# Gate and up projections of a decoder layer: a fourth pair of k-tiles by seven block products in every other chunk

## The chip, the cores and the metric

The kernel runs on one core of a Trainium2 chip. The metric is the device time of one execution in microseconds (us). Engines are called PE (TensorE matmul), PEld (its weight load), DVE (VectorE), ACT (ScalarE), POOL (GpSimd) and SP (SyncE, which here issues the weight DMAs).

## What is computed

One layer of a hybrid decoder on 256 tokens and 2048 channels, in float32: a half-step SwiGLU feed-forward (FFN), a token mixer (state-space branch and windowed attention, merged and projected), and a second SwiGLU FFN, each followed by a LayerNorm. The change touches the first half of both FFNs:

```python
def swiglu(x, w_gate, w_up, w_down):
    return (jax.nn.silu(x @ w_gate) * (x @ w_up)) @ w_down
# D_MODEL = 2048, FFN_HIDDEN = 5632, SEQ = 256, all float32
h = layer_norm(ALPHA * h + 0.5 * swiglu(h, ffn1_w_gate[l], ffn1_w_up[l], ffn1_w_down[l]), ...)
mix = hybrid_mixer(h, ...)
h = layer_norm(ALPHA * h + mix, ...)
h = layer_norm(ALPHA * h + 0.5 * swiglu(h, ffn2_w_gate[l], ffn2_w_up[l], ffn2_w_down[l]), ...)
```

## The kernel before

**Three products for one.** A float32 product is made of three products of rounded parts. For rows `a` and weights `w` the kernel keeps `a_hi`, `a_lo`, `w_hi`, `w_lo` (the rounded value and the rest) and adds `hi*hi + hi*lo + lo*hi` into one PSUM bank. The helper `three` issues these three matmuls, each 128 rows of one token tile by 512 columns.

**Slabs.** Weights stream as slabs of 128 x 2 x 512 (512 KB). SP loads slab n into one of four landing slots (`load`, the DMA is at L540) once the split of slab n-4 is done. ACT rounds it into one of four `w_hi` slots (L1395) when PE has used slab n-4, DVE subtracts to get `w_lo` (L1853) and increments `rest`, on which PE waits. All engines walk through the slabs in the same written-out order.

**Chunks.** The hidden width of 5632 is cut in 11 chunks of 512 columns. A chunk takes 16 slabs: eight pairs of k-tiles, b = 0 to 7, each once for gate and once for up. Chunk 0 (`up_first`) is done with all slabs plain, 12 matmuls each, while the input rows are still being transposed and split on the way in. Chunks 1 to 10 (`up_seven`) do the pairs b in `SEVEN = (2, 4, 6)` by seven block products, the others plainly (24 matmuls a pair).

**Seven products.** Two k-tiles, two token tiles, and gate and up form a 2x2 by 2x2 block product. `seven_products` makes it of 7 products of three matmuls, 21 matmuls instead of 24: two on slab l, two on slab l+1, and three on block sums of the weights. Four bank pairs serve: `own` is the chunk's own PSUM tensor, `aux` the other one (`acc` and `spare` in turn). It needs

- on the rows' side four sums and differences of the row blocks (`s_hi`, `s_lo`), made once per FFN in `up_first`: `mixed_rows`, which is `mixed_of` (L2037 to L2043, on DVE), then `mixed_high` (L1498, ACT), then `mixed_low` (L2071, DVE). They go one set at a time through the scratch rows `sz`, at l = 10, 12 and 14;
- on the weights' side three sums per block: `block_sums` (L2080, L2083, L2085, on DVE) before the two splits, then their rounded part `t_hi` (L1519, ACT, waits until PE has used the previous block's, `t_used`) and the rest `t_lo` (L2090, DVE, increments `t_rest`). There is one `t_hi`/`t_lo`.

**Chunk ends.** At the start of the next chunk ACT copies one shared bank (L1524), `collect` (L2096 to L2098, DVE) takes the shared `aux` banks apart, `sum_chunk` (L2013, L2015) and `product_summed` (L2020) finish the hidden values, PE transposes them (L925), and ACT and DVE split them into `g_hi` (L1477) and `g_lo` (L2028). PE starts a chunk only when `collect` of the previous chunk has freed the banks (`banks_drained`).

**Loops.** Chunks 1 and 2 stand in the open (`ALONE = 2`), chunks 3 to 10 in a loop of four turns with two chunks each; SP has one loop over chunks 1 to 10. In FFN 1, DVE's part of chunk 0 also holds `columns` at l = 7 (small copies of parameters) and `angles` at l = 9 (17 small operations for the rotary positions).

Of the kernel before, what the change touches and what calls it, by code (L numbers as in the profile page):

```python
# [22 lines left out]
ALU = mybir.AluOpType  # L23
# [60 lines left out]

SEVEN = (2, 4, 6)
NC_S = 10
# [9 lines left out]
              for j in range(2)]  # L96
UP_BLOCKS = NC_S * len(SEVEN)
ALL_BLOCKS = UP_BLOCKS + sum(DOWN_BLOCKS)
# [12 lines left out]
MIXED = FFN_MIXED + len(WSO_SEVEN[0])  # L111
ALONE = 2 - NC_S % 2
HIDDEN_AT = 6
# [110 lines left out]

def seven_block(f, i, b):
    return i * len(SEVEN) + ((f - 1) * ALL_BLOCKS - len(SEVEN)) + SEVEN.index(b)

# [75 lines left out]
def build_decoder_layer(nc, x, positions, ffn1_w_gate, ffn1_w_up, ffn1_w_down, ln1_g, ln1_b, w_in, conv_w, conv_b,  # L303
# [20 lines left out]
    with ctx:  # L324
# [201 lines left out]
        def _(sp):  # L526
# [249 lines left out]
        def _(pe):  # L776
# [156 lines left out]

            def seven_products(n, slab_at, l, rows_of, mixed, own, aux, first, last, turned=None):
# [23 lines left out]
            def up_seven_block(f, i, b, own, aux):  # L958
# [103 lines left out]

            def up_seven(f, i, odd):

                own, aux = chunk_banks(odd), chunk_banks(1 - odd)
                banks_drained(f, i)
                for b in range(8):
                    if b == SEVEN[0] and isinstance(i, int) and i == 1:
                        pe.wait_ge(mix_out, (f - 1) * MIXED + len(SEVEN))
                    if b in SEVEN:  # L1070
                        up_seven_block(f, i, b, own, aux)
# [314 lines left out]
        def _(act):  # L1386
# [134 lines left out]
            def copy_one(f, i, odd):  # L1521

                act.wait_ge(t_used, seven_block(f, i, SEVEN[-1]) + 1)
                act.activation(q_one, chunk_banks(1 - odd)[:, 0, :], ACT.Copy).then_inc(q_copied, 1)  # L1524

            def up_seven(f, i, odd):

                for l in range(16):
                    if l == 4 and not (isinstance(i, int) and i == 1):
                        silu_summed(f, i - 1)  # L1530
                    if l == 1 and not (isinstance(i, int) and i == 1):
                        copy_one(f, i - 1, 1 - odd)
                    if l == HIDDEN_AT:
                        hidden_high(f, i - 1, 1 - odd)
                    n = seven_block(f, i, l // 2) if l // 2 in SEVEN else None
                    if n is not None and l % 2 == 0:
                        act.wait_ge(sums, n * 3 + 1)
                    split(f"up{f}", i, l)
                    if n is not None and l % 2 == 1:
                        t_high_part(n)  # L1540

            def ffn(f, ln, cols):
                up_first(f, ln, cols)
                for i in range(1, ALONE + 1):
                    up_seven(f, i, i % 2)
                with act.Fori(1, 1 + (NC_S - ALONE) // 2) as m:
                    for k in range(2):
                        up_seven(f, m * 2 + (ALONE - 1 + k), (ALONE + 1 + k) % 2)
                down(f)
# [8 lines left out]
            def down(f):  # L1558
                for j in range(2):
                    for l, (p, c) in enumerate(DOWN_SLABS[j]):  # L1560
                        s = DOWN_ORDER[j][p]
                        if j == 0 and l == 1:
                            copy_one(f, NC_S, NC_S % 2)
                        if j == 0 and l == 4:
# [282 lines left out]
        def _(dve):  # L1847
# [238 lines left out]

            def t_low_part(n):

                dve.wait_ge(t_high, n + 1)
                dve.tensor_tensor(t_lo[:, :, :], t_sums, t_hi[:, :, :].bitcast(F32), ALU.subtract).then_inc(t_rest, 1)  # L2090

# [25 lines left out]

            def up_seven(f, i, odd):
                for l in range(16):
# [604 lines left out]
```

## Time and profile before

| | us |
|---|---|
| median of 3 runs | 2651.9 (2651.47 to 2652.64) |
| the profiled execution, its own time | 2653.86 |
| span of the profiled execution | 2652.3 |
| PE busy | 2625.4 (99%), 12519 matmuls |
| PEld busy | 2178.3 (82%) |
| DVE busy | 2081.2 (78%) |
| ACT busy | 1378.4 (52%) |
| POOL busy | 128.6 (5%) |
| granted PE clock, mean | 0.998 |

The profile is of one execution. Start times count from the start of its span. In the timeline a row is start, duration, engine, line, operation, what is written from what, how often in a row, and, where the engine was idle before it, how long and who released it. A busy share is an average over the whole span; where an engine is late is seen only in the timeline of one chunk. A matmul's duration is its latency and not what it costs in a row of matmuls: its start to the next one's start is.

### The profile page before, as it was taken

To read this page: it belongs to the slowest core of one execution; us is meant where nothing else is said; L and a number is where in the kernel's file an instruction comes from. 1 tells how busy PE (TensorE), PEld (TensorE's weight loads), DVE (VectorE), ACT (ScalarE), POOL (GpSimd) and SP (SyncE) were. 2 spreads that over 40 slices of the span, in tenths; PEclk is the share of its full clock that TensorE was granted. 3 is DMA by queue.
4 is the path that set the end of the run, shared out by engine and by line. 5 is a ranking of instruction groups with operands and counts; after the bars stand their busy time and mean duration, and the time that the engine had idled before them with its cause. 6 is when DMAs were issued, how large, how long until landed. Compare 5 with 4: busy or idle time off the path is not lost.

```text
span 2652.3 us, 35957 instructions
## 1 busy us (share of the span) xinstructions
PE 2625.4 (99%) x12519; PEld 2178.3 (82%) x12519; DVE 2081.2 (78%) x2372; ACT 1378.4 (52%) x1663; POOL 128.6 (5%) x170
## 2 busy tenths in 40 slices
PE   9999999999999999999999999999999999999997
PEld 7888888888887788888888888788888888888886
DVE  6989989798666665677777765887788989897986
ACT  4555555454444454555665554454465555554553
POOL 1000000000000000211111100000000000000000
PEclk9999999999999999999999999999999999999999
DMA  7666666766655545665655565656666666667564
GB/s 222 196 198 205 192 203 197 229 200 199 200 174 146 158 148 194 206 182 177 185 178 175 177 179 177 210 199 210 212 209 201 190 207 193 202 197 256 190 211 170
DMA packets 286471, 514.03 MB, mean 194 GB/s; under 512 B 19664, under 2 KB 53120, under 8 KB 284320
## 3 DMA queue, kind: packets, MB, share of 16 engines
q1 hardware_dynamic: 279824, 485.03, 58.7%
q0 software_dynamic: 4880, 25.36, 2.6%
q10 hardware_dynamic: 1664, 2.26, 0.2%
q8 instruction: 65, 1.06, 0.2%
q14 instruction: 38, 0.31, 0.0%
HBM read 506.23 MB, written 6.36 MB: 193 GB/s over the span
## 4 chain that ended last, share of the span: by engine, by line
PE 92%; DVE 5%; ACT 1%; DMA 1%; issue 1%; ACTq 0%; POOLq 0%; POOL 0%; SPq 0%; DVEq 0%
PE acc L826 11%; PE acc L828 11%; PE acc L827 11%; PE acc L930 5%; PE acc L932 5%; PE acc L931 5%; PE spare L930 5%; PE spare L931 5%; PE spare L932 5%; PE acc L912 4%; PE acc L913 4%; PE acc L914 4%; PE spare L914 3%; PE spare L912 3%; PE spare L913 3%; PE spare L795 2%
## 5 line engine op out<-in xcount | busy, mean ns | idle before, releaser
L1853 DVE TENSOR_TENSOR w_lo<-land,w_hi 128x1024 fp32r<-128x1024 f32 (+1 forms) x956 | 1150.6, 1222 | 408.2 <-ACT w_hi L1395 399.9
L1395 ACT ACTIVATE w_hi<-land 128x1024 fp32r<-128x1024 f32 (+1 forms) x956 | 965.7, 1026 | 892.9 <-DVE land L2080 293.8
L826 PE MATMUL acc<-w_hi,a_hi 128*128 128x512 f32 (+1 forms) x1168 | 444.1, 380 | 1.8 <-DVE w_lo L1853 1.7
L828 PE MATMUL acc<-w_hi,a_lo 128*128 128x512 f32 (+1 forms) x1168 | 428.8, 367 | 0.0
L827 PE MATMUL acc<-w_lo,a_hi 128*128 128x512 f32 (+1 forms) x1168 | 427.5, 366 | 0.0
L826 PEld LDWEIGHTS acc<-w_hi,a_hi 128*128 128x128 f32 x1168 | 220.4, 189 | 46.2 <-issue 11.0
L828 PEld LDWEIGHTS acc<-w_hi,a_lo 128*128 128x128 f32 x1168 | 220.2, 189 | 37.4
L827 PEld LDWEIGHTS acc<-w_lo,a_hi 128*128 128x128 f32 x1168 | 220.6, 189 | 36.8 <-issue 3.8
L912 PE MATMUL acc<-w_hi,a_hi 128*128 128x512 f32 x512 | 201.6, 394 | 0.7 <-DVE w_lo L1853 0.7
L914 PE MATMUL acc<-w_hi,a_lo 128*128 128x512 f32 x512 | 199.5, 390 | 0.0
L913 PE MATMUL acc<-w_lo,a_hi 128*128 128x512 f32 x512 | 199.5, 390 | 0.0
L2090 DVE TENSOR_TENSOR t_lo<-land,t_hi 128x1536 fp32r<-128x1536 f32 x91 | 159.3, 1751 | 0.3 <-ACT t_hi L1519 0.2
L912 PE MATMUL spare<-w_hi,a_hi 128*128 128x512 f32 x400 | 156.5, 391 | 0.0
L914 PE MATMUL spare<-w_hi,a_lo 128*128 128x512 f32 x400 | 155.8, 389 | 0.0
L913 PE MATMUL spare<-w_lo,a_hi 128*128 128x512 f32 x400 | 155.6, 389 | 0.0
L1519 ACT ACTIVATE t_hi<-land 128x1536 fp32r<-128x1536 f32 x91 | 134.0, 1473 | 0.0
L2080 DVE TENSOR_TENSOR land<-land 128x1024 f32<-128x1024 f32 x91 | 111.0, 1220 | 19.8 <-DMA land<-ffn_w_down 9.8
L930 PE MATMUL spare<-w_hi,g_hi 128*128 128x512 f32 x292 | 114.1, 391 | 0.8 <-DVE w_lo L1853 0.8
L912 PEld LDWEIGHTS acc<-w_hi,a_hi 128*128 128x128 f32 x512 | 96.3, 188 | 21.3 <-DVE w_lo L1853 1.1
L930 PE MATMUL acc<-w_hi,g_hi 128*128 128x512 f32 x292 | 113.7, 389 | 0.0
L932 PE MATMUL spare<-w_hi,g_lo 128*128 128x512 f32 x292 | 113.7, 389 | 0.0
L932 PE MATMUL acc<-w_hi,g_lo 128*128 128x512 f32 x292 | 113.6, 389 | 0.0
(448 smaller groups left out, 4360.9 us busy)
## 6 DMA issues: line engine op xcount, KB each, us to landing
land<-w_in SPq DMA_DIRECT2D x232, 512.0 KB, 3.7
land<-ffn_w_gate SPq DMA_DIRECT2D x176, 512.0 KB, 3.8
land<-ffn_w_up SPq DMA_DIRECT2D x176, 512.0 KB, 4.0
land<-ffn_w_down SPq DMA_DIRECT2D x176, 512.0 KB, 4.6
land<-w_ssd_o SPq DMA_DIRECT2D x64, 512.0 KB, 4.4
land<-w_in SPq DMA_DIRECT2D x132, 128.0 KB, 2.3
land<-w_attn_o SPq DMA_DIRECT2D x32, 512.0 KB, 3.8
land<-w_out SPq DMA_DIRECT2D x32, 512.0 KB, 4.7
```

What stands on the lines that cost most here:

```text
L826: pe.matmul(to, rows_hi, hi, start=first, stop=False)
L827: pe.matmul(to, rows_hi, lo, start=False, stop=False)
L828: mm = pe.matmul(to, rows_lo, hi, start=False, stop=last)
L912: pe.matmul(to, rows_hi, hi, start=first and k == 0, stop=False)
L913: pe.matmul(to, rows_hi, lo, start=False, stop=False)
L914: mm = pe.matmul(to, rows_lo, hi, start=False, stop=last and k == 1)
L930: pe.matmul(to, rows[0], block[0], start=first, stop=False)
L931: pe.matmul(to, rows[0], block[1], start=False, stop=False)
L932: return pe.matmul(to, rows[1], block[0], start=False, stop=last)
L1395: act.activation(w_hi[:, l % SPLIT, 0:deep, 0:width], land[:, l % LAND, 0:deep, 0:width], ACT.Copy).then_inc(high, 1)
L1853: dve.tensor_tensor(w_lo[:, l % SPLIT, 0:deep, 0:width], land[:, l % LAND, 0:deep, 0:width], w_hi[:, l % SPLIT, 0:deep, 0:width].bitcast(F ...
L2090: dve.tensor_tensor(t_lo[:, :, :], t_sums, t_hi[:, :, :].bitcast(F32), ALU.subtract).then_inc(t_rest, 1)
```

## The change

In chunks 1 to 8 the odd ones ("four") take pairs 2, 4, 5, 6 by seven block products, the even ones ("three") 2, 4, 6 as before; chunks 9 and 10 ("last") are as before. There is a second `t_hi`/`t_lo`, and the blocks of chunks 1 to 8 alternate between the two. A fourth set of mixed rows is made in `up_first`, so that `mixed_rows` now stands at l = 8, 10, 12 and 14, ahead of the split of its slab, `mixed_high` at l = 9, 11, 13 and 15 and `mixed_low` two slabs behind its `mixed_rows`. The loop has three turns (chunks 3 to 8), and chunks 9 and 10 stand in the open behind it, on SP also. Waits are the same, with new counts; `t_hi` waits for the block before the previous one where the set allows it. The core of the diff:

```diff
-SEVEN = (2, 4, 6)
+SEVEN = (2, 4, 5, 6)
+UP_SEVEN = {"four": (2, 4, 5, 6), "three": (2, 4, 6), "last": (2, 4, 6)}
+UP_T_SET = {"four": (0, 1, 0, 1), "three": (0, 1, 0), "last": (0, 0, 0)}
+UP_T_FREE = {"four": (0, 1, 1, 1), "three": (1, 1, 1), "last": (0, 0, 0)}
+LOOPED = 8
...
-        s_hi = [placed(f"s_hi{k}", [P, 4, P], F32R, at * K) for k, at in enumerate((88, 90, 92))]
-        s_lo = [placed(f"s_lo{k}", [P, 4, P], F32R, at * K) for k, at in enumerate((94, 86, 42))]
+        s_hi = [placed(f"s_hi{k}", [P, 4, P], F32R, at * K) for k, at in enumerate((88, 90, 92, 40))]
+        s_lo = [placed(f"s_lo{k}", [P, 4, P], F32R, at * K) for k, at in enumerate((94, 86, 42, 84))]
+        t_sets = [(t_hi, t_lo), (placed("t_hi_two", [P, 3, W], F32R, 32 * K), placed("t_lo_two", [P, 3, W], F32R, 76 * K))]
...
                 def t_block(m):
-                    return t_hi[:, m, :], t_lo[:, m, :]
+                    hi, lo = t_sets[t_set]
+                    return hi[:, m, :], lo[:, m, :]
...
-                for i in range(1, ALONE + 1):
-                    up_seven(f, i, i % 2)
-                with pe.Fori(1, 1 + (NC_S - ALONE) // 2) as m:
-                    for k in range(2):
-                        up_seven(f, m * 2 + (ALONE - 1 + k), (ALONE + 1 + k) % 2)
+                for k, kind in enumerate(("four", "three")):
+                    up_seven(f, 1 + k, 1 - k, kind, 0)
+                with pe.Fori(1, LOOPED // 2) as m:
+                    for k, kind in enumerate(("four", "three")):
+                        up_seven(f, m * 2 + (1 + k), 1 - k, kind, m)
+                for i in range(LOOPED + 1, NC_S + 1):
+                    up_seven(f, i, i % 2, "last", i)
...
-            def t_high_part(n):
+            def t_high_part(n, t_set=0, free=0):
                 act.wait_ge(sums, n * 3 + 3)
-                if not is_zero(n):
-                    act.wait_ge(t_used, n)
-                act.activation(t_hi[:, :, :], t_sums, ACT.Copy).then_inc(t_high, 1)
+                if not (isinstance(n, int) and n <= free):
+                    act.wait_ge(t_used, n - free)
+                act.activation(t_sets[t_set][0][:, :, :], t_sums, ACT.Copy).then_inc(t_high, 1)
```

## Rows read from the trace of the kernel before

**Rows 1.** Page, busy time: us, share of the span, instructions
```profile
PE 2625.4 (99%) x12519; PEld 2178.3 (82%) x12519; DVE 2081.2 (78%) x2372; ACT 1378.4 (52%) x1663; POOL 128.6 (5%) x170
```
**Rows 2.** Page, the chain that ended last, by engine
```profile
PE 92%; DVE 5%; ACT 1%; DMA 1%; issue 1%; ACTq 0%; POOLq 0%; POOL 0%; SPq 0%; DVEq 0%
```
**Rows 3.** Busy time by stretch, chunk 3 of FFN 1: window, length, engines, clock, DMA
```profile
144.35:186.74 42.39, 42.39 (x192) 35.17 (x191) 38.30 (x37) 23.07 (x23) 0.00 (x0) 1.00 0.65 199
```
**Rows 4.** Timeline of PE, chunk 3, block b = 4
```profile
166.34 0.39 PE L930 MATMUL spare<-w_hi,s_hi 128*128 128x512 f32 x1
...
169.06 0.39 PE L930 MATMUL acc<-t_hi,s_hi 128*128 128x512 f32 x1
```
**Rows 5.** Timeline of DVE, chunk 3, block b = 4
```profile
159.35 1.22 DVE L2080 TENSOR_TENSOR land<-land 128x1024 f32<-128x1024 f32 x1
160.60 0.69 DVE L2083 TENSOR_TENSOR land<-land 128x512 f32<-128x512 f32 x1
...
164.21 1.75 DVE L2090 TENSOR_TENSOR t_lo<-land,t_hi 128x1536 fp32r<-128x1536 f32 x1
165.88 1.22 DVE L1853 TENSOR_TENSOR w_lo<-land,w_hi 128x1024 fp32r<-128x1024 f32 x1
```
**Rows 6.** Timeline of PE and DVE, down projection of FFN 2
```profile
2505.56 1.75 DVE L2090 TENSOR_TENSOR t_lo<-land,t_hi 128x1536 fp32r<-128x1536 f32 x1
...
2507.46 0.40 PE L930 MATMUL acc<-t_hi,d_hi 128*128 128x512 f32 x1
```
**Rows 7.** Timeline of DVE, chunk 0 of FFN 1
```profile
32.91 2.35 DVE L1853 TENSOR_TENSOR w_lo<-land,w_hi 128x1024 fp32r<-128x1024 f32 x2
...
38.44 1.22 DVE L1853 TENSOR_TENSOR w_lo<-land,w_hi 128x1024 fp32r<-128x1024 f32 x1
39.58 0.68 DVE L2037 TENSOR_TENSOR land<-a_hi,a_lo 128x512 f32<-128x512 f32 x1
...
44.16 0.69 DVE L2071 TENSOR_TENSOR s_lo<-land,s_hi 128x512 fp32r<-128x512 f32 x1
44.95 0.69 DVE L2037 TENSOR_TENSOR land<-a_hi,a_lo 128x512 f32<-128x512 f32 x1
...
51.01 0.69 DVE L2037 TENSOR_TENSOR land<-a_hi,a_lo 128x512 f32<-128x512 f32 x1
...
52.74 1.22 DVE L1853 TENSOR_TENSOR w_lo<-land,w_hi 128x1024 fp32r<-128x1024 f32 x1
```
**Rows 8.** Timeline of PE, slabs 9 and 14 of chunk 0, start of chunk 1
```profile
39.79 0.41 PE L912 MATMUL acc<-w_hi,a_hi 128*128 128x512 f32 x1
...
54.01 0.50 PE L912 MATMUL acc<-w_hi,a_hi 128*128 128x512 f32 x1 [0.25 <-DVE w_lo L1853]
...
59.59 0.39 PE L912 MATMUL spare<-w_hi,a_hi 128*128 128x512 f32 x1
```
**Rows 9.** Timeline of DVE and PE, slab 10 of chunk 0, FFN 2
```profile
1958.11 1.23 DVE L1853 TENSOR_TENSOR w_lo<-land,w_hi 128x1024 fp32r<-128x1024 f32 x1 [1.92 <-ACT w_hi L1395]
...
1961.35 0.39 PE L912 MATMUL acc<-w_hi,a_hi 128*128 128x512 f32 x1
```
**Rows 10.** Timeline of DVE and PE, chunk 1, block b = 4, both FFNs
```profile
78.73 1.75 DVE L2090 TENSOR_TENSOR t_lo<-land,t_hi 128x1536 fp32r<-128x1536 f32 x1
...
84.28 0.39 PE L930 MATMUL acc<-t_hi,s_hi 128*128 128x512 f32 x1
...
1996.81 1.75 DVE L2090 TENSOR_TENSOR t_lo<-land,t_hi 128x1536 fp32r<-128x1536 f32 x1
...
2002.37 0.39 PE L930 MATMUL acc<-t_hi,s_hi 128*128 128x512 f32 x1
```
**Rows 11.** Timeline of DVE, chunk 2: slab 11, and the collection behind it
```profile
125.32 1.23 DVE L1853 TENSOR_TENSOR w_lo<-land,w_hi 128x1024 fp32r<-128x1024 f32 x1 [0.73 <-ACT w_hi L1395]
...
139.76 0.69 DVE L2096 TENSOR_TENSOR resid<-resid,spare 128x512 f32<-128x512 f32 x1 [1.57 <-ACT resid L1524]
```
**Rows 12.** DMA issues: KB each, median us from issue to landing
```profile
land<-ffn_w_gate SPq DMA_DIRECT2D x176, 512.0 KB, 3.8
```

More of the change, by code:

```diff
@@ L96 @@
               for j in range(2)]
-UP_BLOCKS = NC_S * len(SEVEN)
+TWO_CHUNKS = len(UP_SEVEN["four"]) + len(UP_SEVEN["three"])
+UP_BLOCKS = LOOPED // 2 * TWO_CHUNKS + (NC_S - LOOPED) * len(UP_SEVEN["last"])
 ALL_BLOCKS = UP_BLOCKS + sum(DOWN_BLOCKS)
@@ L111 @@
 MIXED = FFN_MIXED + len(WSO_SEVEN[0])
-ALONE = 2 - NC_S % 2
+ALONE = 2
 HIDDEN_AT = 6
@@ L222, in summed_no, with seven_block, chunk_ahead @@
     return i + ((f - 1) * NC_S - 1)
-def seven_block(f, i, b):
-    return i * len(SEVEN) + ((f - 1) * ALL_BLOCKS - len(SEVEN)) + SEVEN.index(b)
+def seven_block(f, kind, m, b):
+    at = (f - 1) * ALL_BLOCKS + UP_SEVEN[kind].index(b)
+    if kind == "last":
+        return at + LOOPED // 2 * TWO_CHUNKS + (m - LOOPED - 1) * len(UP_SEVEN["last"])
+    return m * TWO_CHUNKS + (at + (len(UP_SEVEN["four"]) if kind == "three" else 0))
+def chunk_ahead(kind, m):
+    if kind == "last" and m > LOOPED + 1:
+        return "last", m - 1
+    return ("three", LOOPED // 2 - 1 if kind == "last" else m - 1) if kind != "three" else ("four", m)
 def down_block(f, j, q):
@@ L932, in three, with seven_products @@
                 return pe.matmul(to, rows[1], block[0], start=False, stop=last)
-            def seven_products(n, slab_at, l, rows_of, mixed, own, aux, first, last, turned=None):
+            def seven_products(n, slab_at, l, rows_of, mixed, own, aux, first, last, turned=None, t_set=0):
                 def block(l, k):
@@ L956, in seven_products, with up_seven_block @@
                 three(own[:, 1, :], rows_of(1, 1), t_block(2)).then_inc(t_used, 1)
-            def up_seven_block(f, i, b, own, aux):
+            def up_seven_block(f, i, b, own, aux, kind, at):
                 s = SEVEN.index(b)
@@ L1061, in up_first, with up_seven @@
                         ln_turn(ln, l + 2, x_no)
-            def up_seven(f, i, odd):
+            def up_seven(f, i, odd, kind, at):
                 own, aux = chunk_banks(odd), chunk_banks(1 - odd)
@@ L1069, in up_seven @@
                         pe.wait_ge(mix_out, (f - 1) * MIXED + len(SEVEN))
-                    if b in SEVEN:
-                        up_seven_block(f, i, b, own, aux)
+                    if b in UP_SEVEN[kind]:
+                        up_seven_block(f, i, b, own, aux, kind, at)
                     else:
@@ L1083, in ffn @@
                 up_first(f, ln, x_no)
-                for i in range(1, ALONE + 1):
-                    up_seven(f, i, i % 2)
-                with pe.Fori(1, 1 + (NC_S - ALONE) // 2) as m:
-                    for k in range(2):
-                        up_seven(f, m * 2 + (ALONE - 1 + k), (ALONE + 1 + k) % 2)
+                for k, kind in enumerate(("four", "three")):
+                    up_seven(f, 1 + k, 1 - k, kind, 0)
+                with pe.Fori(1, LOOPED // 2) as m:
+                    for k, kind in enumerate(("four", "three")):
+                        up_seven(f, m * 2 + (1 + k), 1 - k, kind, m)
+                for i in range(LOOPED + 1, NC_S + 1):
+                    up_seven(f, i, i % 2, "last", i)
                 down(f)
@@ L1539, in up_seven @@
                     if n is not None and l % 2 == 1:
-                        t_high_part(n)
+                        k = UP_SEVEN[kind].index(l // 2)
+                        t_high_part(n, UP_T_SET[kind][k], UP_T_FREE[kind][k])
             def ffn(f, ln, cols):
                 up_first(f, ln, cols)
[L1544 to L1548, printed above, removed]
+                for k, kind in enumerate(("four", "three")):
+                    up_seven(f, 1 + k, 1 - k, kind, 0)
+                with act.Fori(1, LOOPED // 2) as m:
+                    for k, kind in enumerate(("four", "three")):
+                        up_seven(f, m * 2 + (1 + k), 1 - k, kind, m)
+                for i in range(LOOPED + 1, NC_S + 1):
+                    up_seven(f, i, i % 2, "last", i)
                 down(f)
@@ L1562, in down @@
                         if j == 0 and l == 1:
-                            copy_one(f, NC_S, NC_S % 2)
+                            copy_one(f, NC_S % 2, "last", NC_S)
                         if j == 0 and l == 4:
@@ L2085, in block_sums, with t_low_part @@
                 dve.tensor_tensor(t_sums[:, 2, :], t_sums[:, 1, :], gate1, ALU.add).then_inc(sums, 1)
-            def t_low_part(n):
+            def t_low_part(n, t_set=0):
+                hi, lo = t_sets[t_set]
                 dve.wait_ge(t_high, n + 1)
-                dve.tensor_tensor(t_lo[:, :, :], t_sums, t_hi[:, :, :].bitcast(F32), ALU.subtract).then_inc(t_rest, 1)
+                dve.tensor_tensor(lo[:, :, :], t_sums, hi[:, :, :].bitcast(F32), ALU.subtract).then_inc(t_rest, 1)
             def collect(f, i, odd):
@@ L2116, in up_first, with up_seven @@
                 mixed_low(f, len(SEVEN) - 1)
-            def up_seven(f, i, odd):
+            def up_seven(f, i, odd, kind, at):
                 for l in range(16):
@@ L2217, in ffn @@
                 up_first(f, ln, cols)
-                for i in range(1, ALONE + 1):
-                    up_seven(f, i, i % 2)
-                with dve.Fori(1, 1 + (NC_S - ALONE) // 2) as m:
+                for k, kind in enumerate(("four", "three")):
+                    up_seven(f, 1 + k, 1 - k, kind, 0)
+                with dve.Fori(1, LOOPED // 2) as m:
                     ch.enter(m, 1, SEVEN_LINKS)
-                    for k in range(2):
-                        up_seven(f, m * 2 + (ALONE - 1 + k), (ALONE + 1 + k) % 2)
-                    ch.leave(1 + (NC_S - ALONE) // 2)
+                    for k, kind in enumerate(("four", "three")):
+                        up_seven(f, m * 2 + (1 + k), 1 - k, kind, m)
+                    ch.leave(LOOPED // 2)
+                for i in range(LOOPED + 1, NC_S + 1):
+                    up_seven(f, i, i % 2, "last", i)
                 down(f)
```

32 lines of the change are left out of this document (17 added, 15 removed).

## The prediction

> **What bounds the kernel now.** I read the page first. PE is busy 99% of the span [rows 1], and the chain of waits that ended last is PE for 92% [rows 2]. So a matmul removed is time gained, as long as PE's operands are ready. Next, busy time by stretch for one chunk of the loop [rows 3]: PE is busy all of its 42.39 us, and DVE 38.30 of them. That is the number to hold on to: DVE has 4.1 us of idle time per chunk, not the 22% that the page's average suggests. ACT has 19 us and plays no part of its own. Then the timelines of PE and DVE side by side, for the lead: how long before PE needs an operand it is ready. In chunk 3 the `t_lo` of block b = 4 ends at 164.21 + 1.75 = 165.96, and the matmul on it starts at 169.06 [rows 4, 5]: a lead of 3.10 us. In the odd chunks of the loop (3, 5, 7 of both FFNs) this lead is 3.10 to 3.13.
>
> **What goes.** From 166.34 to 169.06 lie 12 matmuls [rows 4], so one costs 0.227 us. A seven-product block has 21 and a plain pair 24. One more block in four chunks (1, 3, 5, 7) of two FFNs removes 8 x 3 = 24 matmuls, 5.44 us, or 0.68 us a block. This is all the gain there can be: nothing on PE is added.
>
> **What DVE gets in a loop chunk.** From the start of a block's sums to the end of its `t_lo` DVE takes 165.96 - 159.35 = 6.61 us, of which two splits are there anyhow [rows 5]. Blocks 4, 5 and 6 are now adjacent. The sums of the next block overwrite what `t_lo` reads, so they wait for its end; the second sum, which waits for the first, starts 0.03 after its end (160.60 against 159.35 + 1.22) [rows 5]. So blocks follow each other every 6.64 us on DVE and every 21 x 0.227 = 4.76 us on PE: the lead falls by 1.88 per block. From 3.10 at b = 4 it goes to 1.22 at b = 5 (no stall) and to -0.66 at b = 6. PE stalls there; first at slab 12, whose split is late by nearly as much. A hand-over to a waiting PE costs 0.15 (`t_lo` ended at 2507.31, matmul at 2507.46) [rows 6], and restarting it costs more: from 54.01 to 59.59 lie 24 matmuls, 5.44 by pitch, and it took 5.58 [rows 8]. There the operand was ready at 53.96, so ready to full pace costs 0.05 + 0.14 = 0.19; I take 0.25 for a stall at the block. So each such chunk loses 0.66 + 0.25 = 0.91 and gains 0.68: 0.23 slower. Six chunks: +1.4 us. Bounds: if DVE kept up, -0.68 each (-4.1); if each adjacent block cost DVE 0.4 more than here, 1.0 more to lose in b = 6, +0.6 each (+3.7).
>
> The second set of `t_hi`/`t_lo` makes this possible but gives nothing elsewhere: with one set `t_hi` of b = 5 would wait for the end of b = 4, and before, no wait for `t_used` stood on the path. The SP loads of slabs 10 to 13 are issued at the ends of the splits of slabs 6 to 9, over 6 us before the sums that need them, against 3.8 from issue to landing [rows 12].
>
> A rule of the Trainium skill prices the new wait otherwise. The row says that a DVE operation that waits for the one before starts 0.03 after its end, and the split behind `t_lo`, which doesn't wait, starts at 165.88, 0.08 before its end [rows 5]. The page "VectorE: DVE Perf Modes" (The DRAIN you can't avoid) says that the flush between operations comes regardless and that the semaphore costs nothing extra. By the rule the two hand-overs would save 2 x 0.11, and the six chunks would come to +0.1 instead of +1.4. By the row the wait does cost, and I go by the row.
>
> **The chunk behind it.** DVE starts the collection 3.9 us before the chunk's end instead of 4.6, counted on: behind the stalled `t_lo`, the three splits of slabs 14, 15 and 0, the last of which waits for its load, issued only when slab 12 was split (2.8 before the end of `t_lo`, plus 3.8, plus the 1.06 of ACT). So the even chunk starts with 0.7 less lead on DVE. It has leads of 2.9 there, and its own idle time, 0.73 at slab 11 and 1.57 before the collection [rows 11], takes the 0.7 up again. Nothing is lost, and the next odd chunk starts as before.
>
> **Chunk 1** has no collection in it, and its lead at b = 4 is larger: 84.28 - 80.48 = 3.80 in FFN 1, and 2002.37 - 1998.56 = 3.81 in FFN 2 [rows 10]. Less 3.76 leaves 0.04, a stall of about 0.2: -0.68 + 0.21 = -0.47 each, -0.95 for both.
>
> **Chunk 0: the fourth set of mixed rows.** It is put in front of the others, at l = 8, and here FFN 1 has no room. One `mixed_of` takes 52.74 - 51.01 = 1.73 and one `mixed_low`, up to the next `mixed_of`, 44.95 - 44.16 = 0.79 [rows 7]. Before, the split of slab 9 ended at 38.44 + 1.22 = 39.66 and PE started slab 9 at 39.79 [rows 7, 8]: no lead at all, since `angles` (38.44 - 35.18 = 3.26) is in front of it. Now: split 7 starts at 32.91, `mixed_of` at 34.05, split 8 at 35.78 (ends 37.00, just in time for 39.79 - 2.72 = 37.07), `angles` at 36.92, split 9 from 40.18 to 41.40. PE is 1.6 late. Then `mixed_low` from 41.32, the second `mixed_of` at 42.11, the third 5.37 later at 47.48 (as 39.58 to 44.95), the fourth 6.06 later at 53.54 (as 44.95 to 51.01, with the sines on ACT in it) [rows 7], and split 14 from 55.27 to 56.49. It ended at 53.96. PE ends the chunk 0.19 + 24 x 0.227 later, at 62.12 instead of 59.59 [rows 8]: +2.5 us. Since rounds of 5.4 on DVE face 5.44 on PE, nothing is caught up. Bounds: 0 if the stall were hidden by something, +3.3 if slabs 9 and 10 and the ACT rounds add up instead of overlapping.
>
> In FFN 2 `angles` and `columns` aren't there, and DVE sat idle for 1.92 before split 10, which still ended at 1959.34 against 1961.35 [rows 9]. The 2.52 of new work eats the idle time and then 0.6 to 1.0 of the lead of 2.0. No cost.
>
> **Loops.** One turn fewer in each FFN and two chunks written out. PE shows no gap at the turns before (42.39 us inside the loop [rows 3] and the same in chunk 2 outside it): 0.
>
> **Sum.** 2.5 (chunk 0) - 0.95 (chunks 1) + 1.4 (chunks 3, 5, 7) = +2.95, say +2.9 us. Against the profiled execution's own 2653.86 (its span of 2652.3 and 1.6 around it) that is 2656.8. That execution lay 2.0 over the median of the runs, 2651.9, and the forecast is for the median: 2654.8. About 0.2%, 5.3 us, is what a measurement of this kernel can tell from no change, so my forecast is "same", on the slow side.
>
> **Rivals.**
>
> 1. The full gain: DVE keeps up, PE never waits: 2651.9 - 5.4 = 2646.5. For it: averaged over two chunks DVE would have 38.3 x 2 + 4.3 = 80.9 us of work against 84.1. Against it: leads of 3.10 that fall by 1.88, and slab 9 of chunk 0. Part of it, with chunk 0 hidden and the loop chunks at zero: 2651.
>
> 2. Slower, by the collection. PE may not start a chunk before `collect` has freed the banks. By my times it ends 1.3 us before PE gets there. If the load of slab 0 takes over 5 us instead of 3.8, or ACT's copy queues behind that slab's rounding for longer, the collection comes late and PE waits at each of eight chunk starts, 1.0 each for 2.3 us of delay, which DVE then carries on into block 2. This decides from 1.3 us of delay on: 2654.8 + 8 = 2662.8. For it: ACT does the copy behind the rounding of slab 0. Against it: loads take turns of 2.6 us per slab here and DMA is busy 0.65 [rows 3].
>
> 3. The wait between adjacent blocks is free: the sums start 0.08 before the end of `t_lo`, as the split at 165.88 does, instead of 0.03 after it [rows 5]. The stall at b = 6 falls by 0.22, the loop chunks come to +0.1 in all, and the time to 2653.5, inside my own range. For it stands only that split, which waits for nothing; against it the sum that waits. It is what the page named above would have.
>
> **Chances.** My forecast, within 0.2% with stalls that eat the gain: 0.66. Rival 3: 0.12, also within. Rival 1 in full 0.07, in part (2647 to 2651) 0.05. Rival 2: 0.10. Of the forecast's own 0.66 some 0.04 lies above 2657.2 by a larger cost of chunk 0. Faster by over 0.2% (under 2646.6): 0.07. Slower (over 2657.2): 0.14. Same: 0.79. Range: 2648 to 2659, by the bounds of chunk 0 (+3.3) and of the loop chunks (+3.7, less what they share).
>
> **What the profile of the changed kernel would show.** 12495 matmuls, and 99 `t_lo` instead of 91. The lead at b = 4, 5, 6 of chunk 3: 3.1, 1.2, about 0.15 with a PE idle time of 0.6 or so before slab 12 or the sums, put down to DVE. Chunk 3 at 42.6 us instead of 42.39, chunk 4 unchanged. In chunk 0 of FFN 1 a PE idle time of about 1.6 at slab 9 and 0.9 at slab 10, and chunk 1 starting at 62.1; in FFN 2 none. I am wrong if PE waits for nothing at b = 6, if slab 9 comes on time, or if PE waits at chunk starts.

## The result, and the profile after

| | median, us | runs | ratio [95% interval] |
|---|---|---|---|
| before | 2651.97 | 13 | |
| after | 2659.01 (2657.58 to 2662.65) | 13 | 1.0025 [1.0018, 1.0033] |

The forecast was 2654.8, 2.9 over the time before; the change costs 7.0 us here and 6.6 when both kernels were run again (e8). In the table of experiments e5's ratio leaves out one of its six executions, which took 9414.24 us; its median counts it. The profiled execution took 2659.52 (span 2657.7), at the same granted clock as before, 0.998. The page after, busy time and the chain that ended last, against [rows 1] and [rows 2]:

```profile
span 2657.7 us, 35393 instructions
...
PE 2623.0 (99%) x12495; PEld 2172.4 (82%) x12495; DVE 2116.4 (80%) x2414; ACT 1390.2 (52%) x1673; POOL 129.1 (5%) x170
...
PE 87%; DVE 9%; issue 2%; ACT 1%; DMA 1%; ACTq 0%; DVEq 0%; POOLq 0%; POOL 0%; SPq 0%
```

The 24 matmuls are gone and the span is 5.4 longer; DVE's part of the chain went from 5% to 9%. The next view is what PE waited for (us in total, times, longest):

```profile
PE spare L952 <- DVE w_lo L1881: 5.6, 9, 0.9
PE acc L848 <- DVE w_lo L1881: 3.9, 6, 2.9
PE acc L934 <- DVE w_lo L1881: 2.6, 4, 1.3
```

These three are the blocks of seven products, the projection behind FFN 1 (one wait of 2.9 and five short ones), and chunk 0. Chunk 3 by stretch, against [rows 3]:

```profile
145.78:188.50 42.72, 42.07 (x189) 34.46 (x188) 42.02 (x41) 24.33 (x24) 0.00 (x0) 1.00 0.61 197
```

DVE is busy 42.02 of 42.72 us: the 4.1 of idle time are gone, and PE has 0.65 of it instead. Last, the places on PE's timeline where the difference arises (slabs 9, 10 and 14 of chunk 0, the start of chunk 1, chunk 3 of FFN 1, the projection behind FFN 1, chunk 3 of FFN 2, the down projection of FFN 2):

```profile
40.88 0.50 PE L934 MATMUL acc<-w_hi,a_hi 128*128 128x512 f32 x1 [1.34 <-DVE w_lo L1881]
...
44.52 0.50 PE L934 MATMUL acc<-w_hi,a_hi 128*128 128x512 f32 x1 [0.58 <-DVE w_lo L1881]
...
55.96 0.50 PE L934 MATMUL acc<-w_hi,a_hi 128*128 128x512 f32 x1 [0.22 <-DVE w_lo L1881]
...
61.53 0.39 PE L934 MATMUL spare<-w_hi,a_hi 128*128 128x512 f32 x1
...
178.09 0.50 PE L952 MATMUL spare<-w_hi,s_hi 128*128 128x512 f32 x1 [0.65 <-DVE w_lo L1881]
...
739.17 0.47 PE L848 MATMUL acc<-w_hi,a_hi 128*128 128x512 f32 x1 [2.92 <-DVE w_lo L1881]
...
2098.05 0.50 PE L952 MATMUL spare<-w_hi,s_hi 128*128 128x512 f32 x1 [0.86 <-DVE w_lo L1881]
...
2430.17 0.50 PE L952 MATMUL spare<-w_hi,g_hi 128*128 128x512 f32 x1 [0.82 <-DVE w_lo L1881]
```

PE waits a little in the down projection before, too:

```profile
2424.79 0.50 PE L930 MATMUL spare<-w_hi,g_hi 128*128 128x512 f32 x1 [0.39 <-DVE w_lo L1853]
```

From the first matmul of each chunk here and before I made a ledger of the span:

| stage | difference, us | forecast |
|---|---|---|
| up to slab 7 of chunk 0, FFN 1 | -0.55 | 0 |
| rest of chunk 0, FFN 1 | +2.49 | +2.5 |
| chunk 1, FFN 1 and 2 | -0.52, -0.55 | -0.47 each |
| chunks 3, 5, 7, FFN 1 | +0.35, +0.36, +0.33 | +0.23 each |
| all from there to chunk 1 of FFN 2 | +1.2, of which +2.0 by the idle time at 739.17 | 0 |
| chunks 3 to 8, FFN 2 | +1.5 | +0.7 |
| down projection of FFN 2 | +0.85 | 0 |
| sum | +5.4 | +2.9 |

A second profiled execution of the same kernel (e8, below) has the same waits, and chunks 1 to 10 of both FFNs within 0.03 of these lengths, so these items are not scatter. Two others are: slab 7 of chunk 0 starts 0.15 later there (and up to 1.3 earlier than before in other runs), and the stages between the two FFNs come to +2.6 instead of +1.2, though the long wait in them is 3.00 against 2.92. The ledger can't tell what the change does to these stages beyond that wait. It accounts for the spans, which are 5.4 apart; the medians are 7.0 apart, because the profiled execution of before took 2653.86, 1.9 over its median, and that of the changed kernel 2659.52, 0.5 over.

### The profile page after: what moved, and what is told of

Same layout as the page of the kernel before. It is cut to its first block, busy times and chain, and to the rows that moved or that the text cites. A ratio compares the mean times of both kernels' runs of the same rounds, so it can differ in the third digit from the quotient of the medians.

```text
span 2657.7 us, 35393 instructions
## 1 busy us (share of the span) xinstructions
PE 2623.0 (99%) x12495; PEld 2172.4 (82%) x12495; DVE 2116.4 (80%) x2414; ACT 1390.2 (52%) x1673; POOL 129.1 (5%) x170
## 3 DMA queue, kind: packets, MB, share of 16 engines
q8 instruction: 71, 1.16, 0.2%
## 4 chain that ended last, share of the span: by engine, by line
PE 87%; DVE 9%; issue 2%; ACT 1%; DMA 1%; ACTq 0%; DVEq 0%; POOLq 0%; POOL 0%; SPq 0%
PE acc L848 11%; PE acc L850 11%; PE acc L849 11%; PE acc L952 5%; PE acc L954 5%; PE acc L953 5%; PE spare L952 5%; PE spare L954 5%; PE spare L953 5%; PE acc L934 4%; PE acc L936 4%; PE acc L935 4%; DVE w_lo L1881 3%; PE spare L936 2%; PE spare L934 2%; PE spare L935 2%
## 5 line engine op out<-in xcount | busy, mean ns | idle before, releaser
L2108 DVE TENSOR_TENSOR land<-land 128x1024 f32<-128x1024 f32 x99 | 120.8, 1220 | 14.2 <-DMA land<-w_ssd_o 6.6
L2119 DVE TENSOR_TENSOR t_lo<-land,t_hi 128x1536 fp32r<-128x1536 f32 x75 | 131.3, 1751 | 0.4 <-ACT t_hi L1544 0.2
L934 PE MATMUL spare<-w_hi,a_hi 128*128 128x512 f32 x336 | 131.6, 392 | 0.0
L936 PE MATMUL spare<-w_hi,a_lo 128*128 128x512 f32 x336 | 130.8, 389 | 0.0
L935 PE MATMUL spare<-w_lo,a_hi 128*128 128x512 f32 x336 | 130.8, 389 | 0.0
L953 PE MATMUL spare<-w_lo,g_hi 128*128 128x512 f32 x292 | 113.7, 389 | 0.0
```

What stands on the lines that cost most here:

```text
L934: pe.matmul(to, rows_hi, hi, start=first and k == 0, stop=False)
L935: pe.matmul(to, rows_hi, lo, start=False, stop=False)
L936: mm = pe.matmul(to, rows_lo, hi, start=False, stop=last and k == 1)
L953: pe.matmul(to, rows[0], block[1], start=False, stop=False)
L2119: dve.tensor_tensor(lo[:, :, :], t_sums, hi[:, :, :].bitcast(F32), ALU.subtract).then_inc(t_rest, 1)
```

## Experiments

What was in dispute: which of these items the fourth block causes, and how. Each run is the changed kernel with the edit shown, except e12, which starts from the kernel before; e6 and e11 join earlier edits. "Before beside it" is the kernel before on the same chip.

| run | median | before beside it | ratio [95% interval] |
|---|---|---|---|
| e1_layout | 2653.67 | 2653.38 | 1.0001 [0.9992, 1.0010] |
| e2_mix_only | 2654.96 | 2653.38 | 1.0007 [0.9998, 1.0016] |
| e3_one_set | 2677.14 | 2653.38 | 1.0092 [1.0076, 1.0107] |
| e4_angles_pool | 2658.79 | 2653.38 | 1.0018 [1.0009, 1.0027] |
| e5_product_pool | 2664.9 | 2653.26 | 1.0042 [1.0029, 1.0055] |
| e6_both_pool | 2663.03 | 2653.26 | 1.0036 [1.0023, 1.0049] |
| e7_short_product | 2655.18 | 2653.26 | 1.0007 [0.9998, 1.0016] |
| e8_after_again | 2659.82 | 2653.26 | 1.0025 [1.0014, 1.0036] |
| e9_head_late | 2655.42 | 2653.0 | 1.0009 [1.0000, 1.0018] |
| e10_collect_later | 2659.62 | 2653.0 | 1.0027 [1.0016, 1.0038] |
| e11_all | 2653.16 | 2653.0 | 1.0003 [0.9994, 1.0012] |
| e12_before_mended | 2650.91 | 2653.1 | 0.9992 [0.9983, 1.0001] |

**e1: the new layout and the two sets alone.**

```diff
-SEVEN = (2, 4, 5, 6)
-UP_SEVEN = {"four": (2, 4, 5, 6), "three": (2, 4, 6), "last": (2, 4, 6)}
+SEVEN = (2, 4, 6)
+UP_SEVEN = {"four": (2, 4, 6), "three": (2, 4, 6), "last": (2, 4, 6)}
```

> The changed kernel's loops (three turns of chunks 3 to 8, chunks 9 and 10 written out, SP's loop of two chunks, two t sets in turn) with three blocks in every chunk and three sets of mixed rows: the matmuls of the kernel before in the changed layout. My theory (layout costs nothing; the part of the loss that I did not forecast is where slower code alignment or a late load happens to fall): within 1 us of before, and no long PE idle time at slab 4 of the kv projection behind FFN 1 (0.90 us in the kernel before, 2.92 in the changed one). Rival (the written-out chunks and the longer program cost time behind FFN 1 and in the down projection of FFN 2): 2 to 4 us over before, with the 2.9 us idle at that slab and a second wait at the start of the down projection of FFN 2.

(Not shown: the three blocks of each chunk take the two sets in turn.) No difference that can be measured, and every chunk of FFN 1 starts 0.54 earlier than before, a difference that is there at slab 7 of chunk 0 already. Behind FFN 1 PE waits 1.44, against 0.90 before. The written-out chunks and the second set cost nothing and give nothing.

**e2: e1 and the fourth set of mixed rows, made but not used** (`SEVEN = (2, 4, 5, 6)` again, the blocks as in e1).

> As e1_layout, but with the fourth set of mixed rows made in chunk 0 (and not used). My theory: e1_layout plus 2.2 to 2.5 us, all of it in chunk 0 of FFN 1: PE idle about 1.3 at slab 9 and 0.6 at slab 10; nothing in FFN 2. Rival (the rows are hidden, the blocks cost all of it): e1_layout plus 0.

By the ledger chunk 0 of FFN 1 costs 2.51 here, as in the changed kernel, and little else follows (PE waits 1.39 behind FFN 1, as in e1, against 0.90 before). The term for the fourth set stands alone and is as forecast. The median shows less of it (+1.6), for its first slabs were 1.27 earlier.

**e3: one set for all blocks.**

```diff
-UP_T_SET = {"four": (0, 1, 0, 1), "three": (0, 1, 0), "last": (0, 0, 0)}
-UP_T_FREE = {"four": (0, 1, 1, 1), "three": (1, 1, 1), "last": (0, 0, 0)}
+UP_T_SET = {"four": (0, 0, 0, 0), "three": (0, 0, 0), "last": (0, 0, 0)}
+UP_T_FREE = {"four": (0, 0, 0, 0), "three": (0, 0, 0), "last": (0, 0, 0)}
```

> The changed kernel with one t set for all blocks. My theory: rounding the sums of b = 5 waits until PE is through with b = 4, then 1.47 (ACT) and 1.75 (DVE) face 2.72 of PE work, a stall of 0.5 to 0.9 at b = 5 and as much at b = 6, where 0.9 is lost already by DVE being late: 0.7 to 1.5 more per odd chunk, 6 to 11 us over the changed kernel. Rival (DVE alone sets the pace, the second set is worth nothing): within 1 us of the changed kernel.

17.8 us slower than the changed kernel (0.0067 x 2652), about twice what I expected. Each odd loop chunk of FFN 1 takes 2.4 more than before, 2.0 to 2.1 more than in the changed kernel, and chunk 1 takes 2.8 more than there. DVE and PE in chunk 3 of e3:

```profile
172.95 2.35 DVE L1881 TENSOR_TENSOR w_lo<-land,w_hi 128x1024 fp32r<-128x1024 f32 x2
177.24 1.76 DVE L2119 TENSOR_TENSOR t_lo<-land,t_hi 128x1536 fp32r<-128x1536 f32 x1 [1.94 <-ACT t_hi L1544]
...
179.06 0.50 PE L952 MATMUL acc<-t_hi,s_hi 128*128 128x512 f32 x1 [0.71 <-DVE t_lo L2119]
...
183.07 0.50 PE L952 MATMUL spare<-w_hi,s_hi 128*128 128x512 f32 x1 [1.68 <-DVE w_lo L1881]
```

ACT may not write `t_hi` of b = 5 while PE uses that of b = 4, so DVE stands idle for 1.94 in a row of blocks where it has no time to spare. PE loses 0.71 at b = 5, within the 0.5 to 0.9 expected, and DVE's delay goes on to b = 6, where PE waits 1.68 instead of 0.65. So both waits that I had expected are there; their sum, 1.7 more of idle time and the restarts, is over the 0.7 to 1.5 that I gave. In chunk 1, where the changed kernel has no such wait, b = 6 waits 1.48 in full.

**e4: `angles` on POOL, ahead of chunk 0.**

```diff
-                    if f == 1 and l == 9:
-                        angles()
+            def angles():
...
+            angles()
             def load_rows(dst, gain, bias, arrived):
```

(The part left out of the cut is the same arithmetic on POOL, with each fused operation as two.)

> The changed kernel with the rotary angles (17 small operations, 3.26 us on DVE at slab 9 of chunk 0 in FFN 1) on POOL. My theory: the stalls at slabs 9 and 10 (1.34 and 0.58 of idle time, 2.2 us of the loss in chunk 0) go, the time falls by 2 to 2.5 us from the changed kernel; the stalls at b = 6 stay. Rival (the ACT and DVE rounds of mixed rows set the pace of chunk 0, not the angles): the time falls by less than 0.7 us.

Between slab 7 and slab 14 of chunk 0 PE waits no more; at slab 14 0.55 is left, and the ledger's second item is +0.25 instead of +2.5: its price was the fourth set *together with* `angles`, which stands on the same slabs. Yet the median gains 2 us at most (1.0018 against 1.0025 in e8, intervals that overlap). The ledger shows where it goes: of the 2.4 that e4 is ahead at chunk 8, only 0.7 is left at the start of FFN 2; 0.6 goes behind FFN 1, where PE now waits 3.53 instead of 2.92, and the rest lies in the stages that move by as much from one execution to the next. The wait needed a run of its own (e9).

**e5: the product of silu and up (`product_summed`) on POOL in both FFNs.**

```diff
-                dve.tensor_tensor(prod, silu_t, prod, ALU.mult).then_inc(prod_done, 1)
+                    pool.tensor_tensor(prod, silu_t, prod, ALU.mult).then_inc(prod_done, 1)
```

> The changed kernel with the product of the hidden values (1.22 us on DVE in every chunk, before the block b = 2) on POOL. My theory (PE stalls at b = 6 because DVE's lead of 3.1 at b = 4 falls by 1.88 twice): DVE gains 1.14 of lead, -0.66 turns to +0.48, the idle time of 0.65 before slab 12 of the odd chunks goes, and the time falls by 6 x 1.0 = about 6 us from the changed kernel; PE's transposes get the product some 1.6 us later and still in time. Rival (POOL's 128x1024 operation, some 2.8 us, slows DVE beside it by as much as it saves): 0 to 2 us less, the stalls at b = 6 stay.

It was to take 1.22 us per chunk off DVE, and made it later. DVE and POOL in chunk 3 of e5:

```profile
147.78 1.22 DVE L1891 TENSOR_TENSOR w_lo<-land,w_hi 128x1024 fp32r<-128x1024 f32 x1
148.92 3.42 DVE L2113 TENSOR_TENSOR land<-land 128x1024 f32<-128x1024 f32 x1
```

```profile
148.01 3.25 POOL L709 TENSOR_TENSOR resid<-resid 128x1024 f32<-128x1024 f32 x1 [38.93 <-DVE resid L2053]
```

```profile
178.44 0.50 PE L962 MATMUL spare<-w_hi,s_hi 128*128 128x512 f32 x1 [1.51 <-DVE w_lo L1891]
```

The sum that DVE issues beside the POOL product takes 3.42 instead of 1.22, up to 1.08 after POOL's end (148.01 + 3.25 = 151.26). So DVE loses 2.2 to save 1.22; the lead at b = 4 is 2.25 instead of 3.11, and the wait at b = 6 1.51 instead of 0.65. Against an expected gain of 6 us the kernel is 4.5 slower than the changed one (1.0042 against 1.0025), worse than my rival too. The trace agrees with the Trainium skill, page "GPSIMD Engine Reference" (Key points), which says that GpSimd shares its SBUF interfaces with VectorE and contends with VectorE instructions that have two SBUF inputs. It holds for the operation issued while POOL's was running; the split at 147.78, begun 0.23 before it and with two SBUF inputs as well, kept its 1.22.

**e6: e4 and e5 together.**

> Product and rotary angles on POOL: the version that should beat both. My theory: the 24 matmuls come through in full (-5.4 from the kernel before), with 0.4 left at slab 14 of chunk 0: 4 to 5 us under the kernel before. Rival (POOL beside DVE costs as much): 4 to 5 us over it, as with the angles alone.

1.4 us less than e5 without its long execution (2664.42), about what e4 gives; the two add up and e5's loss stays. I had expected 4 to 5 us under the kernel before, and it is 9.8 over it.

**e7: the product shortened.** It is formed for one eighth of the columns; the kernel leaves out the rest, so its hidden values are not the layer's and only its time is of use.

```diff
-                dve.tensor_tensor(prod, silu_t, prod, ALU.mult).then_inc(prod_done, 1)
+                dve.tensor_tensor(prod[:, :, 0:64], silu_t[:, :, 0:64], prod[:, :, 0:64], ALU.mult).then_inc(prod_done, 1)
```

> The changed kernel with the product of the hidden values formed for one eighth of the columns only (the rest of the hidden values is left out): DVE about 1.0 us shorter per chunk, nothing added on POOL. My theory: as with the product on POOL, about 6 us under the changed kernel, no stall at b = 6. Rival (the stall comes from ACT's rounding or from the loads): no change.

The product and the wait at b = 6, in chunk 3 of e7:

```profile
150.00 0.28 DVE L2048 TENSOR_TENSOR resid<-resid 128x128 f32<-128x128 f32 x1
```

```profile
177.41 0.39 PE L954 MATMUL spare<-t_hi,a_lo 128*128 128x512 f32 x1
177.69 0.50 PE L952 MATMUL spare<-w_hi,s_hi 128*128 128x512 f32 x1
...
181.99 0.39 PE L952 MATMUL spare<-t_hi_two,a_hi 128*128 128x512 f32 x1
```

With 0.94 less on DVE the lead at b = 4 is 3.87 instead of 3.11, the wait of 0.65 is gone but for 0.05 between these two matmuls (0.28 apart instead of 0.227), and the odd loop chunks of FFN 1 are 0.40 faster than before instead of 0.35 slower (those of FFN 2 by 0.19 and twice 0.37). That is the change's mechanism shown from the other side: three matmuls less are worth having as soon as DVE has a microsecond more. The whole is 4.6 us faster than the changed kernel beside it (e8), where I had expected about 6. The gain of a chunk is not the full 0.68: the 19 matmuls from the first of these rows to the last take 4.58 where 19 x 0.227 = 4.31, and 0.27 is what is missing.

**e8: the changed kernel again**, for a second profile.

> The changed kernel once more, for its profile: are the idle times of 2.9 us at slab 4 behind FFN 1 and of 0.8 at the start of the down projection of FFN 2 its own, or do they change from one execution to the next? My theory: the second is DMA under full load and moves by some tenths; the first hangs on how long ACT's issue of a small load takes (0.4 in one profile, 3.3 in the other) and changes. Rival (they come with four blocks per odd chunk): the same again within 0.2.

Same time, same places: 3.00 at the projection behind FFN 1, 0.86 in the down projection. So my theory that the first changes from one execution to the next is wrong, and the rival holds: both come with this kernel.

**e9: three small loads on ACT's queue (`dt_bias`, `a_log`, `d_skip`, 32 KB each) issued at slab 8 of the projection behind FFN 1, instead of before slab 4.**

```diff
-            for k, src in enumerate((dt_bias, a_log, d_skip)):
-                act.dma_start(head_r[:, k, :], src[0].partition_broadcast(P)).then_inc(row_in, 16)
+                if l == 8:
+                    for k, src in enumerate((dt_bias, a_log, d_skip)):
+                        act.dma_start(head_r[:, k, :], src[0].partition_broadcast(P)).then_inc(row_in, 16)
```

> The changed kernel with ACT's three small loads behind FFN 1 (head_r) issued before slab 8 of the kv projection instead of before slab 4. Theory (the 2.9 and 3.0 us of PE idle time at slab 4 come from the first of them, whose issue holds ACT for 3.3 us where it held it 0.4 in the kernel before): the idle time at slab 4 goes, and the time falls by 1.5 to 3 us from the changed kernel. Rival (ACT would have waited anyway, for the loads of the kv weights under full DMA): the idle time stays, no change.

ACT behind FFN 1, first in the kernel before, then after, then in e9:

```profile
728.32 0.40 ACTq L1586 DMA_DIRECT2D head_r<-dt_bias  x1
728.75 0.81 ACTq L1586 DMA_DIRECT2D head_r<-a_log  x1
729.59 0.96 ACTq L1586 DMA_DIRECT2D head_r<-d_skip  x1
...
734.72 0.47 PE L826 MATMUL acc<-w_hi,a_hi 128*128 128x512 f32 x1 [0.90 <-DVE w_lo L1853]
```

```profile
730.75 3.27 ACTq L1614 DMA_DIRECT2D head_r<-dt_bias  x1
734.06 0.46 ACTq L1614 DMA_DIRECT2D head_r<-a_log  x1
734.55 0.45 ACTq L1614 DMA_DIRECT2D head_r<-d_skip  x1
735.05 1.02 ACT L1448 ACTIVATE a_hi<-spare,ln_col 128x256 fp32r<-128x256 f32 x2 [3.90 <-issue]
```

```profile
736.55 0.40 ACTq L1616 DMA_DIRECT2D head_r<-dt_bias  x1
736.98 0.45 ACTq L1616 DMA_DIRECT2D head_r<-a_log  x1
737.46 0.45 ACTq L1616 DMA_DIRECT2D head_r<-d_skip  x1
```

In the changed kernel the first issue holds ACT's sequencer for 3.27 instead of 0.40, and the roundings of the next slabs queue behind it. From the start of the first issue to the end of the third it is 2.23 before and 4.25 after (735.00 - 730.75), and PE then waits 0.90 and 2.92: the issues less 1.33 in both. The same holds, within 0.02, in each of the nine other runs that issue them there: e1 2.78 and 1.44, e2 2.72 and 1.39, e3 3.51 and 2.19, e4 4.86 and 3.53, e5 4.47 and 3.13, e6 3.71 and 2.37, e7 3.98 and 2.66, e8 4.35 and 3.00, e10 3.80 and 2.46. Later, in e9, each takes 0.40 to 0.45 and PE doesn't wait there. So the issue is the cause, worth 2.0 against before. The whole is 4 us faster than the changed kernel, more than the 1.5 to 3 expected.

The wait of 0.82 at 2430.17 (0.39 before) is gone in e9 as well, though nothing was changed near it. ACT's rows there, before and after, show what it is:

```profile
2418.50 1.06 ACT L1395 ACTIVATE w_hi<-land 128x1024 fp32r<-128x1024 f32 x1 [6.12 <-DMA land<-ffn_w_down]
```

```profile
2423.95 1.06 ACT L1420 ACTIVATE w_hi<-land 128x1024 fp32r<-128x1024 f32 x1 [6.99 <-DMA land<-ffn_w_down]
```

The first slabs of the down projection wait for their loads. The load comes 5.45 later than before where PE is 4.55 late: 0.9 is lost to the transfer. Why it lands later in some kernels than in others I can't say.

What stretches the issue behind FFN 1 stays open too. The first one grows where four blocks are used and not with the mere layout or the mixed rows (e1, e2: 0.39 and 0.40; there the third takes 1.16 and 1.55 instead of 0.96, and the wait is 1.44 and 1.39), but not with the delay: e3, the slowest, has 2.40, and e4, which gets there earlier than the changed kernel, 3.91. Busy DMA engines alone don't explain it either: behind the last of POOL's four stores of 512 KB (`kept`, issued at 730.44, and 0.3 before ACT's first issue in before too) their share is 0.87 over 730 to 735 in the changed kernel, and 0.96 over 727 to 732 in the kernel before, where that issue takes 0.40. At e9's later place it is 0.31 (736 to 738).

**e10: the collection a slab later, behind a "three" chunk's end, to use DVE's idle time elsewhere.**

```diff
-                    if l == 1 and not (isinstance(i, int) and i == 1):
+                    if l == (2 if kind == "four" else 1) and not (isinstance(i, int) and i == 1):
-                    elif l == 1:
+                    elif l == (2 if kind == "four" else 1):
```

> The changed kernel with ACT's copy and DVE's collection behind the split of slab 1, not ahead of it, at the start of chunks 3, 5 and 7, where DVE waits 1.57 to 1.7 us for the copy. Theory (the lead that DVE has at b = 4 is set by when it comes free after the collection): the split fills the wait, the lead at b = 4 rises from 2.9 or 3.1 by 1.1, the idle time before slab 12 goes (six times 0.65 to 0.85 of idle, 1.0 with what lies around it), and the time falls by 4 to 6 us. Rival (PE now waits for the collection at the chunk start, or the DVE time comes back elsewhere): 0 to 2 us slower than the changed kernel.

No gain (1.0027, where I had expected 4 to 6 us less), and the lead at b = 4 is 3.14, as good as unchanged. DVE of e10 at the start of chunk 3:

```profile
139.48 1.23 DVE L1881 TENSOR_TENSOR w_lo<-land,w_hi 128x1024 fp32r<-128x1024 f32 x1 [0.50 <-ACT w_hi L1420]
140.69 0.69 DVE L2125 TENSOR_TENSOR resid<-resid,spare 128x512 f32<-128x512 f32 x1
...
143.87 1.23 DVE L1881 TENSOR_TENSOR w_lo<-land,w_hi 128x1024 fp32r<-128x1024 f32 x1 [0.51 <-ACT w_hi L1420]
145.49 1.22 DVE L2041 TENSOR_TENSOR resid<-resid,acc 128x1024 f32<-128x1024 f32 x1 [0.40 <-PE acc L936]
```

The last row says why: `sum_chunk` needs PE's last matmul of the chunk before. DVE can't run ahead past that point, whatever is moved before it, so its lead into the blocks is pinned by PE. Work behind that row counts (as the product does, e7).

**e11: e4, e9 and e10 together.**

> Both, and the rotary angles on POOL: the version that should beat both kernels. Theory: the effects add: 24 matmuls fewer (-5.4 from the kernel before), +0.6 left in chunk 0 and the two chunks 1, and about -1 from the small loads: 4.5 to 6 us under the kernel before. Rival (the stages' losses hide one another): within 2 us of the kernel before.

The changed kernel so mended is back at the time of before, as my rival had it, and not 4.5 to 6 us under it.

**e12: the kernel before, with e4's and e9's edits.**

> The kernel before with the two mends of the last version (rotary angles on POOL, the small loads behind FFN 1 issued before slab 8): the control for it, three blocks in every chunk and no fourth set of mixed rows. Theory (in the loop chunks a fourth block costs about 0.3 more than it saves, in chunk 1 it saves 0.5): the mends give the kernel before 1.0 to 1.8 us (0.9 idle at slab 4 and some tenths in chunk 0), so this is the fastest of all, about 1 to 2 us under the mended changed kernel. Rival (the blocks do gain once the side costs are gone): it is slower than the mended changed kernel.

The fastest of all: 2650.91, ratio 0.9992 [0.9983, 1.0001], a gain of 2 us that the interval doesn't quite separate from nothing. PE waits neither at slab 14 of chunk 0 (0.25 before) nor behind FFN 1 (0.90 before). It is 2.2 us under e11 by the medians, which were taken on different chips and whose intervals against before overlap. (The spans are only 0.6 apart: slab 7 of chunk 0 came 1.0 earlier in e11.) By the ledgers of the two, chunk 0 from slab 7 on takes 1.0 more in e11 (the fourth set), and the chunks behind it 0.4 more in FFN 1 and 0.5 in FFN 2 (the blocks). So the fourth block costs about 2 us with its side effects mended; the whole is at the edge of what the medians can tell.

## Why the prediction was right, and where it was short

The sign is right. The time is 4.2 us above the figure that I gave and on the very edge of the range (2659.01 against 2659). It is also over the 2657.2 up to which I had called the result "same", with a chance of 0.79; what came had 0.14, and the interval [1.0018, 1.0033] sets it apart from no change. The mechanism in chunks 0, 1, 3, 5 and 7 is as I had it. That the sum stays at the edge is partly luck: of the ledger's 5.4, 2.0 and 0.85 stand in places that I had put at nothing, the slabs before slab 7 take 0.55 off, and the range was wide for other terms. Point by point:

- **Chunk 0, +2.5.** Right in size and in place: idle 1.34 at slab 9 (said: 1.6) and 0.58 at slab 10 (0.9), and 2.49 in all by the ledger; e2 shows it alone, e4 removes it.
- **FFN 2, chunk 0: nothing.** Right: PE doesn't wait there.
- **Chunk 1, -0.47.** Right: -0.52 and -0.55.
- **Chunks 3, 5, 7: the wait was found, its size was too small**, 0.23 against +0.35 in FFN 1 and +0.57, +0.39 and +0.39 in FFN 2 (with 0.04 more in each even chunk there). The lead at b = 5 came out at 1.22, as worked out, and PE's wait is at slab 12, as said. DVE in chunk 3 of the changed kernel shows what was missing:

```profile
165.62 1.75 DVE L2119 TENSOR_TENSOR t_lo_two<-land,t_hi_two 128x1536 fp32r<-128x1536 f32 x1
167.41 1.22 DVE L2108 TENSOR_TENSOR land<-land 128x1024 f32<-128x1024 f32 x1
...
172.27 1.75 DVE L2119 TENSOR_TENSOR t_lo<-land,t_hi 128x1536 fp32r<-128x1536 f32 x1
174.22 1.23 DVE L2108 TENSOR_TENSOR land<-land 128x1024 f32<-128x1024 f32 x1 [0.20 <-DVE t_lo L2119]
```

  PE's first matmuls on the `t_lo` of b = 4 and b = 5 in chunk 3, and DVE's second hand-over in chunk 1:

```profile
170.48 0.39 PE L952 MATMUL acc<-t_hi_two,s_hi 128*128 128x512 f32 x1
...
175.24 0.39 PE L952 MATMUL acc<-t_hi,s_hi 128*128 128x512 f32 x1
```

```profile
87.31 1.75 DVE L2119 TENSOR_TENSOR t_lo<-land,t_hi 128x1536 fp32r<-128x1536 f32 x1
89.10 1.23 DVE L2108 TENSOR_TENSOR land<-land 128x1024 f32<-128x1024 f32 x1
```

  The first hand-over takes 0.04 (167.41 after 167.37), the second 0.20 (174.22 after 174.02), so the lead falls by 1.88 and then by 2.05. I had put 0.03 on both from one row [rows 5]. From 3.11 the lead thus comes to -0.82 instead of -0.66, and the stall costs 0.35 + 0.68 = 1.03 in all, 0.21 over that, where I took 0.25. That is the whole excess of FFN 1. Over six chunks the term is 2.5 instead of 1.4. All nine kernels with four blocks have the 0.20 in every odd loop chunk, and 0.03 to 0.04 in chunk 1 (89.10 after 89.06), which has the same blocks and stands outside the loop. So three adjacent blocks don't make the 0.16; what in the loop does isn't shown. In FFN 2 chunk 3 is also 0.24 longer than in e9 (42.98 against 42.74); that stays open.
- **The step that failed: that nothing follows outside the chunks with four blocks.** 2.0 more of idle time behind FFN 1 (shown by e9) and 0.85 in the down projection of FFN 2 (a late load; there in e4, e8 and e10, 0.17 and 0.25 in e2 and e11, and gone in e1, e3, e5, e6, e7, e9 and e12, so it is tied to no one edit). I had priced the stages that the diff touches, by DVE and PE, and no DMA issue on ACT's queue. The trace of before had a hint that I didn't follow: PE is idle for 0.90 in that place.
- **Two slips that change nothing in the sum.** The upper bound of the loop chunks: 0.4 more on each of two adjacent blocks is 0.8, so +1.0 a chunk and +6.2 for six, not +0.6 and +3.7. And the 0.15 of a "hand-over to a waiting PE" [rows 6]: that matmul has no idle time before it, so the row doesn't show one. At slab 12 of chunk 3, where PE does wait, it starts at 178.09, some 0.05 after the split's end.
- **The rivals.** The full gain (rival 1): refuted, PE waits at b = 6 in all six loop chunks. The late collection (rival 2): did not occur; PE doesn't wait at chunk starts, and the collection's place doesn't matter (e10). The free hand-over (rival 3): refuted, by 0.04 and 0.20 instead of -0.08. It is what the rule of the Trainium skill, page "VectorE: DVE Perf Modes" (The DRAIN you can't avoid), would give; the trace doesn't bear the rule out here.
- **The second set gives nothing by itself** (e1), and makes the fourth block bearable: right, though its worth was about twice the figure that I gave before e3.

## What to carry to other kernels

An average of 78% busy hid that DVE had only 4 us to spare per chunk, and loses 1.88 to 2.05 of a lead of 3.1 with each further block in a row: work out the lead and what each block takes from it, and look at which point the lead is pinned (here PE's last matmul of a chunk). Three matmuls saved are worth 0.68, and the stall that they bring here costs 1.03. Follow the small waits that PE has already: one of 0.9 behind FFN 1 grew to 2.9 by a change elsewhere, and went when three DMA issues were moved; that mend and the one of `angles` made the kernel before 2 us faster by its median (interval up to 1.0001), without a fourth block.

## What was not expected of the hardware

- A DMA issue of 32 KB on ACT's queue took 0.39 to 0.40 us at best and 2.40 to 3.91 in eight profiles of seven kernels behind FFN 1 (2.40, 2.48, 2.81, 3.00, 3.27, 3.38, 3.51, 3.91), with ACT's computing queued behind it.
- One POOL operation of 3.25 us beside a DVE operation with two SBUF inputs lengthened that one from 1.22 to 3.42 when it was issued during it, and not when it had begun 0.23 before.
- A DVE operation that waits for the one before it began 0.03 to 0.04 after its end in one place of the chunk, and 0.20 in another, the same in nine kernels; outside the loop the second place too took 0.03 to 0.04.
